# A mixture-of-experts loop skewed by one product, its first weight loads in smaller pieces, and a new ending

## The chip, the core and the metric

The kernel runs on one core of a Trainium2 chip. The core has TensorE for matrix products (the profile calls its matmuls PE and its weight loads PEld), VectorE (DVE), ScalarE (ACT), GpSimd (POOL) and SyncE (SP, which here only issues transfers). The metric is the device time of one execution in microseconds (us), taken as a median of several runs. The engines run side by side and meet at semaphores, so the time is that of the longest chain of waits and not a sum of work.

## What is computed

One layer of a decoder for 256 prompt tokens and 8 x 8 sample tokens, 320 in all, of width 1024. A mixer (a short convolution and four heads of a linear recurrence) comes first, then 32 experts of which each token uses 4, then a last RMSNorm. Cut to what the change touches:

```python
mix = jnp.concatenate([y_conv, o], axis=-1) @ w_out
x = x + mix
# channel mixer, on t = rmsnorm(x)
for e in range(N_EXPERTS):                       # 32
    a = jnp.minimum(t @ w_gate[e] + b_gate[e], SWIGLU_LIMIT)
    u = jnp.clip(t @ w_up[e] + b_up[e], -SWIGLU_LIMIT, SWIGLU_LIMIT)
    hid = (u + 1.0) * a * jax.nn.sigmoid(SWIGLU_ALPHA * a)
    y = y + combine[:, e:e + 1] * (hid @ w_down[e] + b_down[e])
...
y_prompt, y_sample = rmsnorm(x + y, final_norm_w)
```

Every expert has three float32 matrices of 1024 x 1024, 4 MiB each: 96 matrices and 403 MB in all, which the kernel reads once from HBM.

## The kernel before

**Weights.** The matrices go through a ring in SBUF of five places, called groups 0 to 4, of four slots (1 MiB) each. Matrix i goes to group i % 5. Before, i counts gate, up, down of expert 0, then of expert 1, and so on. SP issues all loads in that order from one queue; for matrix i it waits on `wUsed`, which TensorE raises after each quarter of a product, until matrix i-5 (or the half of it) has been used. Matrices 5 to 11 and the last twelve are loaded in halves, the very last in a half and two quarters. The groups overlap older data: group 3 (slots 4 to 7) holds the output projection `w_out` until the mixer's last product, and the end of group 4 holds `mixT`, the mixer's result turned. The first loads therefore wait for the mixer: matrix 0 and 1 on projections that have used their slots (`projMM`), the first half of matrix 4 on `stSMM` and others, matrix 3 and the second half of matrix 4 on `woutMM`, the end of the output projection.

**One expert on TensorE** (lines 1446 to 1476). `product(0, ...)` is gate and `product(1, ...)` is up: 16 float32 products (8 tiles of the contraction by two column halves) at line 1428 after a bias product at line 1411. Inside gate, after its second, third and fourth quarter, stand the three parts of `scatter` (line 1402), which returns the rows of the expert before to their tokens. After up comes `gather` (lines 1319 and 1322), which picks the 64 token rows of the next expert, then the transpose of `hid` (line 1471), `turn_gates` (1384) and `turn` (1390) for the next expert, and last `product(2, ...)`, down, of the same expert.

**Around it.** DVE makes `ga`, `gt`, `gu`, `hid` and adds scattered rows to x (line 985). The output of down is split into three bf16 parts so that `scatter` can be bf16: ACT copies the high part (line 632, `yHigh`), DVE subtracts (991), ACT copies the middle part (634), DVE makes the low part (994).

**The ending** (lines 1495 to 1516, 641 to 655, 1055 to 1062). All engines first pass `further_rounds`, an If that would run more rounds if an expert had over 64 tokens; it isn't taken. Then TensorE scatters the last expert's three parts (1503), spreads `final_norm_w` from `parRows` over all partitions with 32 small products (1511, 1513) and folds the sample tokens' sums (1084). DVE adds (1058) and scales by root and weight (1053). ACT loads the square root's table and makes the squares (648) and the roots (655). SP writes the outputs (400, 403).

Of the kernel before, what the change touches and what calls it, by code (L numbers as in the profile page):

```python
# [5 lines left out]
def hybrid_shortconv_hgrn2_moe_step(nc, A):  # L6
# [9 lines left out]
    D = 1024  # L16
# [29 lines left out]
    ML = 3 * PER_LOOP  # L46
    HALVES_TO, HALVES_FROM = 12, MATS - 12

    def buf(j):

        return (0, 1, 0, 1, 2)[(j - FIRST) % PER_LOOP]

    def buf_before(j):

        return buf(j - 1) if j else buf(E - 1)
# [39 lines left out]
    with ctx:  # L95
# [32 lines left out]
        mixT = view(R2, 0, "p (k t) -> p k t", shape=(8, NT), k=8)  # L128
# [18 lines left out]
        hidT, gt, hid, yrest = ga, gs, gu, xgs  # L147
        ysb = R1[:, 4608:5120].bitcast(bf16).rearrange("p (s d) -> p s d", s=2)
        ysb = [ysb[:, 0, :], ysb[:, 1, :], R4[:, 2400:2656].bitcast(bf16)]
        cv = view(R4, 0, "p (c t) -> p c t", shape=(4, NT), c=4)  # L150
# [4 lines left out]
        PT = R4[:, 1920:2400].bitcast(bf16).rearrange("p (n t) -> p n t", n=3)  # L155
# [15 lines left out]
        gates = sb("gates", [128, 3, 3])  # L171
        rw = sb("rw", [128, 8, E])
        rb = sb("rb", [128, E])
        parRows = sb("parRows", [60, 128])
# [18 lines left out]
        eh = sb("eh", [128, 3, SLOTS], bf16)  # L193
# [7 lines left out]
        endIn = sem("end_in")  # L201
        xIn = [sem(f"x_in{b}") for b in range(3)]
# [7 lines left out]
        woutMM, x2TMM, lgMM, posMM = sem("wout_mm"), sem("x2T_mm"), sem("lg_mm"), sem("pos_mm")  # L210
# [22 lines left out]
        posShift, moeDone, finDone, normed = sem("pos_shift"), sem("moe_done"), sem("fin_done"), sem("normed")  # L233
        lastMM, fnwMM = sem("last_mm"), sem("fnw_mm")
        yHigh, yRest, yMid, yLow = sem("y_high"), sem("y_rest"), sem("y_mid"), sem("y_low")
        aloneP, aloneV, aloneT = sem("alone_pool"), sem("alone_dve"), sem("alone_pe")
# [42 lines left out]
        def further_rounds(eng, one_round, close_round=lambda r: None, rounds=None):  # L279

            rounds = count_of_rounds(eng) if rounds is None else rounds
            with eng.If(rounds > 1):
# [8 lines left out]
                eng.nop()  # L291
            with eng.Else():
                eng.nop()
# [5 lines left out]
        def _(sp):  # L299
# [46 lines left out]
            for i in range(2):  # L346
                for before in range(GROUP_AT[i], GROUP_AT[i] + 4):
                    sp.wait_ge(projMM, load_done(before))
                load_matrix(i, 0, i)
# [5 lines left out]
            load_half(4, 1, 1, 0)  # L355
            sp.wait_ge(s0Out, 16)
            sp.wait_ge(biasDone, 1)
            load_matrix(2, 0, 2)
            sp.wait_ge(woutMM, 3)
            load_matrix(3, 1, 0)  # L360
            load_half(4, 1, 1, 1)

            for i in range(NG_, MATS):
                e, m = i // 3, i % 3
# [15 lines left out]
                if i % ML == 3 * FIRST - 1 and 3 * FIRST < i < MATS - 1:  # L380
                    sp.sem_inc(endIn, 16)

            sp.wait_ge(roundsDone, 1)
            def all_loads(r):
                for i in range(3 * FIRST):
                    sp.wait_ge(wUsed, r * (LPE * E) + 4 * max(0, i - NG_ + 1) + START)
                    load_matrix(i, i // 3, i % 3)
                with sp.Fori(0, LOOPS) as it:
                    for n in range(ML):
                        i = 3 * FIRST + n  # L390
                        sp.wait_ge(wUsed, r * (LPE * E) + it * (4 * ML) + (4 * (i - NG_ + 1) + START))
                        load_matrix(i, it * PER_LOOP + i // 3, i % 3)
                    sp.sem_inc(endIn, 16)

            further_rounds(sp, all_loads)
            yp = A["y_prompt"][0].rearrange("(b p) d -> b p d", p=128)
            ys = A["y_sample"].rearrange("s t d -> (s t) d")
            for b in range(2):
                sp.wait_ge(finDone, b + 1)
                sp.dma_start(yp[b], yout[:, b, :]).then_inc(yOut, 16)  # L400
            sp.wait_ge(finDone, 3)
            for half in range(2):
                sp.dma_start(ys[:, HALF * half:HALF * half + HALF], yout[64 * half:64 * half + 64, 2, 0:HALF]).then_inc(yOut, 16)
# [7 lines left out]
        def _(pool):  # L411
# [22 lines left out]
            def one_round(r):  # L434
# [3 lines left out]
                for j in range(FIRST):  # L438
                    pool.wait_ge(wUsed, r * (LPE * E) + LPE * j + START)
# [1122 lines left out]
```

## Time and profile before

| | |
|---|---|
| median of three runs | 1128.1 us (1128.0 to 1129.16) |
| the profiled execution's own time | 1130.27 us |
| its span | 1128.4 us |
| PE busy | 1103.0 us (98%) |
| DVE, ACT, POOL busy | 394.5, 162.7, 18.2 us |
| moved | 431.67 MB, mean 383 GB/s |
| waits of PE at line 1428 for DMA | 11.7 us |

PE's busy time says that it always had something under way, not that it was at its peak. The slices of the page show where the transfers ran: the first fifth of the span has gaps, and from then on every slice but the last stands near 430 GB/s.

### The profile page before, as it was taken

The page shows a single profiled execution, that of the slowest core. Times are in us where ns is not written, and L with a number is a line of the kernel's source. Part 1 is how long each engine was busy: PE and PEld are TensorE (multiplying, and loading weights), DVE is VectorE, ACT ScalarE, POOL GpSimd, SP SyncE. Part 2 cuts the span into 40 slices and gives each one's busy share as a digit, 9 for nine tenths or more (in the row PEclk, how much of TensorE's full clock was granted, in tenths as well). Part 3 has the DMA queues.
Part 4 walks back from the last instruction along what each step waited for, and adds up shares of the span by engine and source line. Part 5 has one row for each costly group of instructions (what it writes and reads, how often), then busy time and mean ns, then how long its engine had stood idle before and what let it go on. Part 6 is the DMA issues. An engine that isn't in the chain of part 4 may idle for free.

```text
span 1128.4 us, 15518 instructions
## 1 busy us (share of the span) xinstructions
PE 1103.0 (98%) x6341; PEld 454.0 (40%) x6341; DVE 394.5 (35%) x703; ACT 162.7 (14%) x284; POOL 18.2 (2%) x45
## 2 busy tenths in 40 slices
PE   8999999999999999999999999999999999999997
PEld 5657754433333333333333333333333333333333
DVE  4165385433333333333333333333333333233233
ACT  3100124211111111111111111111111111111102
POOL 0002000000000000000000000000000000000000
PEclk9999999999999999999999999999999999999997
DMA  9970247999999999999999999999999999999991
GB/s 323 333 227 22 129 159 298 396 428 427 436 428 430 432 432 433 429 432 433 432 430 432 432 432 432 431 432 432 433 431 431 432 433 429 429 429 428 427 423 63
DMA packets 41442, 431.67 MB, mean 383 GB/s; under 512 B 3809, under 2 KB 23069, under 8 KB 26431
## 3 DMA queue, kind: packets, MB, share of 16 engines
q1 hardware_dynamic: 40592, 430.38, 91.3%
q10 hardware_dynamic: 815, 0.82, 0.2%
q8 instruction: 22, 0.36, 0.1%
q14 instruction: 13, 0.11, 0.0%
HBM read 427.48 MB, written 3.71 MB: 382 GB/s over the span
## 4 chain that ended last, share of the span: by engine, by line
PE 79%; DMA 19%; DVE 1%; ACT 0%; issue 0%; SPq 0%; DVEq 0%
PE ps L1428 47%; DMA ring<-in_w_gate 15%; PE ps L1135 9%; PE ps L1402 5%; DMA ring<-in_w_up 4%; PE ps L1254 3%; PE ps L1319 3%; PE ps L1411 2%; PE ps L1322 1%; PE ps L1390 1%; PE ps L1471 1%; PE ps L1125 1%; PE ps L1384 1%; DMA x<-in_x_sample 0%; PE ps L1511 0%; PE ps L1513 0%
## 5 line engine op out<-in xcount | busy, mean ns | idle before, releaser
L1428 PE MATMUL ps<-ring,RT 128*64 128x512 f32 x3072 | 689.8, 594 | 11.7 <-DMA ring<-in_w_gate 10.3
L1428 PEld LDWEIGHTS ps<-ring,RT 128*64 128x64 f32 x3072 | 210.5, 137 | 410.3 <-issue 381.7
L985 DVE SCALAR_TENSOR_TENSOR x<-ps,gates,x 128x1024 f32<-128x1024 f32 (+1 forms) x93 | 102.9, 1106 | 127.6 <-PE ps L1402 126.5
L1135 PE MATMUL ps<-R,ring 128*128 128x320 f32 x384 | 107.5, 436 | 0.3 <-issue 0.3
L991 DVE TENSOR_TENSOR RT<-ps,R 128x512 f32<-128x512 f32 x32 | 22.1, 692 | 228.9 <-ACT R L632 228.9
L1135 PEld LDWEIGHTS ps<-R,ring 128*128 128x128 f32 x384 | 71.8, 190 | 31.2 <-issue 1.8
L1402 PE MATMUL ps<-R 64*128 64x512 bf16 x558 | 76.8, 381 | 0.0
L1025 DVE TENSOR_SCALAR RT<-ps 128x512 f32<-128x512 f32 x32 | 22.1, 692 | 143.1 <-PE ps L1428 143.1
L624 ACT ACTIVATE RT<-RT 128x512 f32<-128x512 f32 x32 | 20.2, 630 | 300.1 <-DVE RT L1019 300.1
L1402 PEld LDWEIGHTS ps<-R 64*128 64x128 bf16 x558 | 20.8, 98 | 86.0 <-issue 50.3
L603 ACT ACTIVATE RT<-ps 128x512 f32<-128x512 f32 x33 | 19.7, 597 | 237.1 <-PE ps L1322 237.1
L632 ACT ACTIVATE R<-ps 128x512 bf16<-128x512 f32 x32 | 19.1, 597 | 228.3 <-PE ps L1428 228.3
L1319 PE MATMUL ps<-R,P 128*64 128x512 bf16 x396 | 50.6, 389 | 0.0
L973 DVE TENSOR_TENSOR RT<-ps,par 128x512 f32<-128x512 f32 x33 | 22.8, 692 | 67.8 <-PE ps L1390 67.8
L1411 PE MATMUL ps<-R,eh 128*64 128x512 bf16 x192 | 38.9, 401 | 0.2 <-issue 0.2
L1319 PEld LDWEIGHTS ps<-R,P 128*64 128x64 bf16 x396 | 22.2, 109 | 34.7 <-issue 19.3
L1254 PE MATMUL ps<-ring 128*128 128x512 f32 (+1 forms) x96 | 35.9, 598 | 0.0
L1022 DVE TENSOR_TENSOR RT<-RT 128x512 f32<-128x512 f32 x32 | 22.2, 692 | 25.0 <-ACT RT L624 25.0
L994 DVE TENSOR_TENSOR R<-RT,R 128x512 bf16<-128x512 f32 x32 | 22.2, 693 | 22.3 <-ACT R L634 22.3
L1322 PE MATMUL ps<-R,P 128*64 128x256 bf16 x396 | 28.0, 275 | 0.0
L1322 PEld LDWEIGHTS ps<-R,P 128*64 128x64 bf16 x396 | 22.2, 108 | 8.0 <-issue 0.4
L1390 PE MATMUL ps<-consts,RT 128*128 128x128 f32 x132 | 24.7, 310 | 0.0
(226 smaller groups left out, 559.2 us busy)
## 6 DMA issues: line engine op xcount, KB each, us to landing
ring<-in_w_gate SPq DMA_DIRECT2D x26, 4096.0 KB, 32.5
ring<-in_w_up SPq DMA_DIRECT2D x25, 4096.0 KB, 32.0
ring<-in_w_down SPq DMA_DIRECT2D x25, 4096.0 KB, 32.8
ring<-in_w_up SPq DMA_DIRECT2D x14, 2048.0 KB, 39.0
ring<-in_w_down SPq DMA_DIRECT2D x13, 2048.0 KB, 39.8
ring<-in_w_gate SPq DMA_DIRECT2D x12, 2048.0 KB, 40.8
ring<-in_w_in SPq DMA_DIRECT2D x14, 1024.0 KB, 12.7
ring<-in_w_out SPq DMA_DIRECT2D x4, 1024.0 KB, 10.0
```

What stands on the lines that cost most here:

```text
L973: TT(xgT.rearrange("p (c a s) -> p c a s", c=4, a=2), ps[:, 3, :].rearrange("p (c a s) -> p c a s", c=4, a=2), par[:, NG:NG + 8].rearrange ...
L985: STT(xb[b], rows, gates[:, par, b:b + 1], xb[b], ALU.mult, ALU.add).then_inc(accDone, 1)
L994: TT(ysb[2], yrest, ysb[1], ALU.subtract).then_inc(yLow, 1)
L1022: TT(gt, ga, gs, ALU.mult).then_inc(tDone, 1)
L1135: ins = MM(ps[:, n % 2, 0:NT], slot_k(L, 256)[:, k, 128 * half:128 * half + 128], hT[:, k, :], start=(k == 0), stop=(k == KT - 1))
L1254: ins = MM(dst, mixT[:, k, t0:t0 + n], w[:, 512 * half:512 * half + 512], start=(k == 0), stop=(k == KT - 1))
L1319: ins = MM(in_fours(to), P[:, b, 0:SLOTS], half_of(h2p[part][b], half), start=(b == 0 and part == 0), stop=False)
L1322: ins = MM(in_fours(to[:, 256 * at:256 * at + 256]), P[:, 2 + at, 0:SLOTS], half_of(h2p[part][2], half), start=False, stop=(part == 2 and ...
L1390: ins = TR(ps[:, 3, 128 * c:128 * c + 128], fourth(xgs, c), ident)
L1402: ins = MM(to, PT[64 * half:64 * half + 64, par, t0:t0 + n], ysb[part][64 * half:64 * half + 64, :], start=(part == 0), stop=(part == 2))
L1411: MM(shape(ps[64 * half:64 * half + 64, bank, :]), eh[:, buf(j), :], cols(bias3[:, mat, :], half), start=True, stop=False)
L1428: ins = MM(shape(ps[64 * half:64 * half + 64, bank, :]), lhs(k), cols(w, half), start=False, stop=(k == KT - 1))
```

## The change

1. **Order of the matrices** (`I_GATE`, `I_UP`, `I_DOWN`). They are now counted and loaded as gate 0, up 0, gate 1, up 1, down 0, gate 2, up 2, down 1, ..., gate 31, up 31, down 30, down 31.
2. **Skewed loop.** One step on TensorE is gate e and up e with `gather` for e+1, down of expert e-1 with `turn_gates` and `turn` inside it, and the transpose of hid e. The scatter inside gate e is that of expert e-2. ACT, DVE and POOL follow. `hidT`, `gates`, `PT` and `eh` move or have five buffers.
3. **First loads.** Matrix 1 goes in two halves, each as soon as its two slots are free. Matrix 4 (now down 0) has three quarters early and the fourth after the output projection; for this the first two tiles of `mixT` lie elsewhere. Matrix 3 (now up 1) goes in quarters: three as the output projection frees the slots of `w_out` (`woutFree`), one at its end.
4. **Ending.** The last expert's output is copied once in float32 (`yLast`, with `PTLast` for its places) and scattered by 6 float32 products in place of 18 bf16 ones. `final_norm_w` comes by DMA to all partitions, three loads into a free slot. The steps after the rounds stand inside the If, on its first side, and once more after the other rounds.

The core of the diff:

```diff
+    I_GATE, I_UP, I_DOWN = [0] + [3 * j - 1 for j in range(1, E)], [1] + [3 * j for j in range(1, E)], [3 * j + 4 for j in range(E - 1)] + [MATS - 1]
...
-            with eng.If(rounds > 1):
+            with eng.If(rounds < 2):
+                ending()
+                eng.nop()
+            with eng.Else():
...
-            load_half(4, 1, 1, 0)
+            load_half(4, *matrix_of(4), 0)
+            load_quarter(4, *matrix_of(4), 2, lateIn[4])
             sp.wait_ge(s0Out, 16)
             sp.wait_ge(biasDone, 1)
-            load_matrix(2, 0, 2)
+            load_matrix(2, *matrix_of(2))
+            for n, arrived in enumerate((groupIn[3], quarterIn[0], lateIn[3])):
+                sp.wait_ge(woutFree, n + 1)
+                load_quarter(3, *matrix_of(3), n, arrived)
             sp.wait_ge(woutMM, 3)
-            load_matrix(3, 1, 0)
-            load_half(4, 1, 1, 1)
+            load_quarter(3, *matrix_of(3), 3, quarterIn[1])
+            load_quarter(4, *matrix_of(4), 3, quarterIn[2])
...
+                sp.wait_ge(wUsed, 4 * NEXT + START)
+                sp.dma_start(fnw[0], A["final_norm_w"].partition_broadcast(128)).then_inc(fnwIn, 16)
...
+                        gate_up(e, m, j, it, [lambda: None] + [lambda b=b: scatter(b, e2, m2, buf(j - 2)) for b in range(3)] if j > 1 else [])
+                        down(before, j - 1, it, [lambda: turn_gates(after), lambda: turn(after)])
+                        turn_hidden(e)
...
+                down(e0 + (E - 1), E - 1, 0, [lambda b=b: scatter(b, e0 + (E - 2), p0 + (E - 2), buf(E - 2)) for b in range(3)])
+                pe.wait_ge(ptLastOut, r + 1)
+                pe.wait_ge(yHigh, e0 + E + START)
...
+                act.activation(yLast, ps[:, 2, :], ACT.Copy).then_inc(yHigh, 1)
```

**The loop on TensorE.** Before, the second half of one expert, from the bias of up to the end of down (L1428 is a matrix's products, 16 to a matrix; L1319 and L1322 gather; L1471, L1384 and L1390 are transposes):

```order
L1411 MATMUL ps<-R,eh 64x512 x2
L1428 MATMUL ps<-ring,RT 64x512 x16
L1372 REGISTER_ALU
L1319 MATMUL ps<-R,P 64x512 x12
L1322 MATMUL ps<-R,P 64x256 x12
L1471 MATMUL ps<-consts,RT 128x128 x4
L1384 MATMUL ps<-identb,P 128x128 x2
L1384 MATMUL ps<-identb,P 128x64
L1390 MATMUL ps<-consts,RT 128x128 x4
L1411 MATMUL ps<-R,eh 64x512 x2
```

After, the same place, from gather to the transposes of hid (L1382 and L1385 are gather, L1496 the products of down, L1447 and L1453 the two turns, L1534 the transpose of hid):

```order
L1382 MATMUL ps<-R,P 64x512 x12
L1385 MATMUL ps<-R,P 64x256 x12
L1478 MATMUL ps<-R,eh 64x512 x2
L1496 MATMUL ps<-ring,R 64x512 x4
L1447 MATMUL ps<-identb,P 128x128 x2
L1447 MATMUL ps<-identb,P 128x64
L1496 MATMUL ps<-ring,R 64x512 x4
L1453 MATMUL ps<-consts,RT 128x128 x4
L1496 MATMUL ps<-ring,R 64x512 x8
L1534 MATMUL ps<-consts,RT 128x128 x4
```

Down follows gather at once and is broken in two places; the transpose of hid stands behind it.

**The ending on DVE.** Before, the last three adds (L1058) stand behind the way past the If's body:

```order
L1040 TENSOR_SCALAR posm<-posm 128x99
L1041 ISA
L1042 ISA
L285 UNCONDITIONAL_BRANCH
L289 UNCONDITIONAL_BRANCH
L284 REGISTER_ALU
L284 COMPARE_AND_BRANCH
L282 UNCONDITIONAL_BRANCH
L292 UNCONDITIONAL_BRANCH
L1058 SCALAR_TENSOR_TENSOR x<-ps,gates,x 128x1024 x2
L1058 SCALAR_TENSOR_TENSOR x<-ps,gates,x 128x512
L1052 RECIPROCAL st<-st 128x1
```

After, the adds of the last two experts (L1044) come ahead of the one branch, and the scaling (L1120, L1122) right behind it:

```order
L1103 REGISTER_ALU
L1103 COMPARE_AND_BRANCH
L1044 SCALAR_TENSOR_TENSOR x<-ps,R,x 128x1024 x2
L1044 SCALAR_TENSOR_TENSOR x<-ps,R,x 128x512
L1044 SCALAR_TENSOR_TENSOR x<-ps,R,x 128x1024 x2
L1044 SCALAR_TENSOR_TENSOR x<-ps,R,x 128x512
L296 COMPARE_AND_BRANCH
L1120 RECIPROCAL st<-st 128x1
L1122 SCALAR_TENSOR_TENSOR R<-x,st,ring 128x1024
```

The adds moved ahead of the branch, and the weight is read from the ring and no longer from PSUM.

## Rows read from the trace of the kernel before

**Rows 1.** The page: span, and GB/s moved in 40 equal slices of it

```profile
span 1128.4 us, 15518 instructions
GB/s 323 333 227 22 129 159 298 396 428 427 436 428 430 432 432 433 429 432 433 432 430 432 432 432 432 431 432 432 433 431 431 432 433 429 429 429 428 427 423 63
```

**Rows 2.** The chain that ended last: start, length in us, what; middle of the span

```profile
660.09 6.87 PE ps L1428 x32
...
687.81 6.87 PE ps L1428 x32
...
750.43 41.31 DMA ring<-in_w_gate
...
808.71 41.32 DMA ring<-in_w_gate
```

**Rows 3.** Timeline of SP's issues, 150 to 225 us: start, length, line, destination and source

```profile
177.16 0.33 SPq L304 DMA_DIRECT2D ring<-in_w_down  x1
198.16 0.33 SPq L304 DMA_DIRECT2D ring<-in_w_gate  x1
198.60 0.37 SPq L311 DMA_DIRECT2D ring<-in_w_up  x1
212.60 3.76 SPq L311 DMA_DIRECT2D ring<-in_w_down  x2
```

**Rows 4.** Windows around the first product: length; engines' busy us; last: clock, DMA share, GB/s

```profile
198.00:212.60 14.60, 13.66 (x117) 6.83 (x117) 9.59 (x32) 6.81 (x14) 0.00 (x0) 1.00 0.92 380
212.60:232.00 19.40, 19.40 (x111) 8.44 (x109) 4.29 (x9) 2.15 (x4) 0.00 (x0) 1.00 1.01 429
```

**Rows 5.** Timeline of PE at the first product of expert 0

```profile
208.95 3.62 PE L1428 MATMUL ps<-ring,RT 128*64 128x512 f32 x16
```

**Rows 6.** Line 316, the issue of the last quarter, and its time to landing

```profile
L316 SPq DMA_DIRECT2D ring<-in_w_down x1: 3887/3887/3887, 1059.2 to 1059.2; - x1
...
DMA to landing us min/median/max: 44.3/44.3/44.3
```

**Rows 7.** Timeline of PE in gate of expert 31, where it last waits for gate's second half

```profile
1083.96 1.51 PE L1428 MATMUL ps<-ring,RT 128*64 128x512 f32 x6 [0.48 <-DMA ring<-in_w_gate]
```

**Rows 8.** The chain that ended last, experts 29 and 31, with PE's last wait at 1093.76

```profile
1025.79 0.76 PE ps L1402 x6
1026.54 1.87 PE ps L1428 x8
...
1093.76 3.65 PE ps L1428 x16
1097.42 1.36 PE ps L1319 x12
...
1099.45 0.68 PE ps L1471 x4
1100.13 0.24 PE ps L1384 x3
...
1101.39 6.89 PE ps L1428 x32
```

**Rows 9.** Timeline of all engines in the ending, with idle time before in brackets

```profile
1108.31 0.60 ACT L632 ACTIVATE R<-ps 128x512 bf16<-128x512 f32 x1 [7.13 <-PE ps L1428]
...
1111.06 1.28 ACT L572 ACT_TABLE_LOAD   x1 [0.77 <-issue]
...
1113.67 3.13 DVE L1058 SCALAR_TENSOR_TENSOR x<-ps,gates,x 128x1024 f32<-128x1024 f32 x3 [2.53 <-issue]
...
1114.99 1.06 ACT L648 ACTIVATE R<-x 128x1024 f32<-128x1024 f32 x1 [2.43 <-DVE x L1058]
...
1121.27 0.16 DVE L1052 RECIPROCAL st<-st 128x1 f32<-128x1 f32 x1 [4.46 <-PE ps L1513]
...
1124.24 0.75 DVE L1053 SCALAR_TENSOR_TENSOR R<-x,st,ps 128x512 f32<-128x512 f32 x1
1125.02 1.21 SPq L403 DMA_DIRECT2D y_sample<-R  x2
```

More of the change, by code:

```diff
@@ L201, in hybrid_shortconv_hgrn2_moe_step @@
         endIn = sem("end_in")
+        quarterIn = [sem(f"quarter_in{n}") for n in range(3)]
         xIn = [sem(f"x_in{b}") for b in range(3)]
@@ L290, in further_rounds @@
                         eng.nop()
-                eng.nop()
-            with eng.Else():
+                ending()
                 eng.nop()
@@ L404, in _ @@
+            further_rounds(sp, all_loads, ending=outputs)
             sp.wait_ge(yOut, 64)
@@ L1065, in _ @@
+            further_rounds(dve, one_round, rounds=rounds[0], ending=scales)
         @block.tensor
@@ L1078, in _ @@
             pe.wait_ge(parIn, 16)
[L1079 removed]
+            TR(ps[:, 0, 0:52], parRows[:], ident[0:52, 0:52]).then_inc(parMM, 1)
             def sum_halves(column, out):
@@ L1445, in one_round, with gate_up, down @@
                     stay_busy(3)
+                def gate_up(e, m, j, it, between=()):
+                    pe.wait_ge(ehDone, m + 1 + START)
+                    pe.wait_ge(xgTOut, m + 1 + START)
+                    pe.wait_ge(aDone, e + START)
+                    product(0, half_c(xgT), I_GATE[j], it, buf(j), between)
+                    pe.wait_ge(uDone, e + START)
+                    product(1, half_c(xgT), I_UP[j], it, buf(j))
+                    gather(m + 1)
+                def down(e, j, it, between):
+                    pe.wait_ge(yRest, e + START)
+                    product(2, half_c(hidT), I_DOWN[j], it, buf(j), between, operand=(hidTOut, e + 1 + START))
@@ L1446, in experts, with turn_hidden @@
+                def turn_hidden(e):
+                    pe.wait_ge(hidDone, e + 1 + START)
+                    pe.wait_ge(hidTOut, e + START)
+                    for c in range(4):
+                        ins = TR(ps[:, 4, 128 * c:128 * c + 128], fourth(hid, c), ident)
+                    ins.then_inc(hidTMM, 1)
+                gate_up(e0, p0, 0, 0)
+                turn_hidden(e0)
+                turn_gates(p0 + 1)
+                turn(p0 + 1)
                 def experts(it, these):
                     for j in these:
-                        e = e0 + (it * PER_LOOP + j)
@@ L1461, in experts @@
-                        pe.wait_ge(xgTOut, m + START)
-                        pe.wait_ge(aDone, e + START)
-                        product(0, 0, half_c(xgT), e, it, j, [lambda: None] + [lambda b=b: scatter_before(b) for b in range(3)]
-                                if not isinstance(e, int) or e > 0 else [])
-                        pe.wait_ge(uDone, e + START)
-                        product(1, 1, half_c(xgT), e, it, j)
-                        gather(m)
-                        pe.wait_ge(hidDone, e + 1 + START)
@@ L1469, in experts @@
-                        pe.wait_ge(hidTOut, e + START)
-                        for c in range(4):
-                            ins = TR(ps[:, 4, 128 * c:128 * c + 128], fourth(hid, c), ident)
-                        ins.then_inc(hidTMM, 1)
-                        turn_gates(m)
-                        turn(m)
-                        pe.wait_ge(yRest, e + START)
-                        product(2, 2, half_c(hidT), e, it, j, operand=(hidTOut, e + 1 + START))
-                experts(0, range(FIRST))
+                        e, m = e0 + (it * PER_LOOP + j), p0 + (it * PER_LOOP + j)
@@ L1507, in _ @@
-            FN = 52
-            for k in range(D // 128):
-                row = ident[0:FN + 8, FN + k:FN + k + 1]
-                at = 128 * (k % 4)
-                MM(ps[:, 4 + k // 4, at:at + 128], row.broadcast_to([FN + 8, 128]), parRows[:], start=True, stop=True)
-                half = slice(64 * (k // 4), 64 * (k // 4) + 64)
-                ins = MM(ps[half, 2, at:at + 128], row.broadcast_to([FN + 8, 64]), parRows[:], start=True, stop=True)
-            ins.then_inc(fnwMM, 1)
-            pe.wait_ge(finSq, 3)
```

328 lines of the change are left out of this document (180 added, 148 removed).

## The prediction

> **What bounds the kernel now.** I read the page's GB/s line first. 96 matrices of 4.19 MB are 403 MB of the 432 MB moved, and from the ninth slice to the last but one the line stands at 423 to 436 [rows 1]: up to about 1101 us the transfers don't pause. The page's PE line says 98% busy as well, so the next view is the chain, to see who waits. In its middle one expert follows another after 687.81 - 660.09 = 27.72 us with no DMA piece: there TensorE waits for nothing and eats what the ring holds. From 750 us on the chain runs through loads, and two of its DMA pieces that lie six matrices apart are 58.28 us apart [rows 2], 9.71 us a matrix, 29.14 an expert, 4.19 MB / 9.71 = 432 GB/s. So TensorE is 1.4 us an expert faster than the stream, lives off the ring for 500 us and then waits for the stream. The end is set by (a) when the stream starts for good, (b) 91 matrices at its rate, (c) what comes after the last of them.
>
> **Part 1: earlier first loads, worth 0.7 us and not 10.** The diff brings 1 MiB of matrix 4 and 3 MiB of matrix 3 forward into the idle stretch before 198 us. Taken alone that is 4.19 MB / 0.43 = 9.7 us of stream. But the ring has five places, and matrix 5 can only be asked for when TensorE has used half of matrix 0. Before, that issue is at 212.60 [rows 3], 3.65 us after the first product began at 208.95 [rows 5], and that product waits for the routing, not for weights. The loads issued at 198.16 and 198.60 are 6.29 MB; by 212.6 they had moved 14.6 us x 380 GB/s = 5.55 MB [rows 4], so 0.74 MB were left, 1.7 us at 429 GB/s. The stream before was thus only 1.7 us behind "all five places full". After, the places are full some microseconds early, the stream stops, and starts anew at 212.6. How long a start takes I bound from the same row: 5.55 MB at 429 GB/s take 12.9 us of the 14.4 since the issue, so 1.5 us at most, and no less than 0; I take 1.0, nearer the top since the row also has a slow stretch. Everything behind it, the last landing included, comes 1.7 - 1.0 = 0.7 us earlier (0.2 to 1.7). Issue work on SP is 0.33 us for each added load [rows 3], with nothing behind it until 212.6. The skewed order frees the places at nearly the same times: first half of matrix 2 used at about 231 us, while the queue then holds work until 232.8. That margin is thin, and a bubble costs about what it lasts.
>
> The Trainium skill, page "DMA: Bandwidth & Descriptors", section "Specifications", gives about 0.6 us to the first byte on this path; by it the restart is at 213.2 and the shift 1.1 us in place of 0.7.
>
> **Part 2: the skewed loop, dearer for TensorE by 0.3 us an expert, free up to 0.45.** It removes no instruction. Chains that it stretches out (`hid`, `hidT`, the three-way split) weren't waited for before: no such piece stands in the chain's middle. What it adds is that down is broken twice. A quarter of a product is 6.87 / 4 = 1.72 us, but one that follows a scatter takes 1.87 [rows 8]. Two more such entries are 2 x 0.15 = 0.30 us; from below it is 0, if transposes do not cost what scatters do, and from above three entries at 0.17, 0.5. Pace 28.02 us, still under 29.14. Before, expert 1 starts at 208.7 + 27.7 - 2.6 = 233.8 us (expert 0 has no scatter), and 31 experts x 27.72 would have ended at 1093.1, against the real 1108.3: 15.2 us spare. The new order takes 30 x 0.30 = 9.0 of them, and about 1.8 for a later gate 1 and the new end: 4.4 us, 0.15 an expert, are left. So the price is nothing on the path, covered by the stream; if that cover is used up, each further 0.1 us an expert costs 3 us.
>
> **Part 3: where TensorE ends.** The last wait before is for the second half of expert 31's up, at 1093.76, and down ends at 1101.39 + 6.89 = 1108.28 [rows 8]. After, the order of arrival is up 31, down 30, down 31. The place that up 31's second half takes in the stream is the one that gate 31's had, which let PE go on at 1083.96 [rows 7], now 0.7 earlier, 1083.3. Then, from rows 8: second half of up 3.65; gather 2.03; bias 0.23; down 30 with its turns 6.87 + 0.24 + 0.68 + 0.30 = 8.09: it ends at 1097.3. Its output copy (0.60 on ACT [rows 9]) and the hidden copy after the transpose (0.68, then 0.60) must end before down 31 starts: 1.5 us. Down 31 carries the scatter of expert 30 in it: 4 quarters of 1.87 and 3 scatters of 0.76, 9.76. **End 1108.5**, 0.2 later than before. The last quarter lands at 1059.2 + 44.3 = 1103.5 [rows 6] and is needed at 1106.6, so it isn't what is waited for.
>
> **Part 4: the ending, -8.1 us.** Before [rows 9]: the adds start at 1113.67, after 2.53 us in which DVE had nothing to wait for (the way past the If), though the first scatter part was there near 1112. They end at 1116.8. Then DVE idles 4.46 us for the 32 small products of `final_norm_w` (L1513), and scales from 1121.27 to 1124.99; 3.4 us later the span ends. After: `yLast` copy 0.63, to 1109.1; first pair of the float32 scatter 1.0 (the 8 pairs of a matrix take 6.87 us, 0.86 a pair [rows 8], and about 0.15 until DVE sees it; 1.9 if this pair doesn't overlap as those do), to 1110.1; adds 3.13, to 1113.3; the branch not taken 0.15; scaling 3.72, to 1117.1; outputs 3.4: **1120.5**. That is the 4.46 us of idle removed, the adds 3.5 us earlier, less 0.15. What is late next: ACT's first root. Copy end 1109.1, 0.77 issue, table 1.28 and its small use 0.2: 1111.4; square and root take 1.5, 1112.9, half a microsecond before DVE asks. The norm's weights (0.79 MB, 1.8 us) queue behind the last quarter and land at about 1105.5, needed at 1113.4.
>
> Unknown is what the branch costs DVE. Bounds: 0.1, and the 2.53 of rows 9. I take the low end, since the new code stands right behind the branch as the order shows, where the old stood beyond the body. The Trainium skill, "Runtime: NRT & Kernel Launch", section "Instruction fetch mechanics", says that a taken branch out of the fetched window stalls for a fetch; the 2.53 us agree with it, and by it the new branch is free, while SP's jump after its last issue falls beside the outputs' flight.
>
> **The sum.** Span 1128.4 + 0.2 - 8.1 = 1120.5. The execution shown took 1130.27 by its own time, with a span of 1128.4; the median of runs is 1128.1, 0.3 under that span, so I forecast 1128.1 - 7.9 = 1120.2 us.
>
> **The rivals.**
> A. *The early loads pay in full.* If the stream at 212.6 had as much backlog as was brought forward, 9.7 us would come off the stream, but TensorE's spare of part 2 lets only 4.4 of them through: 1120.2 - 4.4 = 1116. Against it: the 0.74 MB left by rows 4. 5%.
> B. *TensorE becomes the bound.* Entries at 0.17 and one more of them (pace 28.2) or small waits eat the 4.4 us spare; at 28.3 the end moves by (0.58 - 0.45) x 30 = 4 us: 1124. For it: the spare is thin. 15%.
> C. *The gain of the ending is half.* The branch or the float32 scatter cost DVE 2.5 us more: 1122.7. 10%.
> D. *Slower: a wait once an expert.* `down(e-1)`, `turn_hidden(e)` and the next gate stand in a row; should gate e+1 have to wait for `xgT`, or its scatter for the low part of the split, by w us each time, the loss is (w - 0.15) x 30. From w = 0.41 on the whole gain is gone, at w = 0.8 the time is 1139. Against it: from the end of down the split takes 0.6 + 0.75 + 0.6 + 0.7 us in sequence with the hidden copy between, some 2.8, and the scatter comes 4.4 us after it. 7%.
> E. *No change.* A bubble near 232 us or at the first whole-matrix load (about 280 us) of some 3 us, with B: 1126 to 1129. 8%.
> Forecast: 55%, with a range of its own of 1118.5 to 1122.5.
>
> **How the numbers follow.** B, C and the forecast lie between 1117.5 and 1124.5 and hold 80%. A little of A reaches down to 1116. The range is 1116.5 to 1125. Faster by over 0.2% (under 1125.8) is the forecast, A, B, C: 85%; within 0.2%, about what a measurement of this kernel can tell from no change: 7%; slower 8%.
>
> **What would show it.** Right: in the changed profile SP's first issue of matrix 5 is still at 212.6, with a hole in GB/s just before it; the pace in the middle is near 28.0; the chain meets DMA pieces later than 750 us, perhaps only from 1000 us on; the last product ends near 1108.5; DVE's idle time before the scaling is under 0.5 us. Wrong: a pace over 28.2, any PE wait for ACT or DVE inside the loop, a GB/s slice under 420 after 212 us, or 2 us of DVE idle between adds and scaling.

## The result, and the profile after

The changed kernel takes 1169.4 us (median of four runs, 1165.5 to 1171.4) against 1128.6 us before (four runs): a ratio of 1.035, 95% interval 1.032 to 1.038. I had forecast 1120.2 and a range of 1116.5 to 1125.0. It is slower by 41 us, and outside of the range. Times here are medians and ratios compare undisturbed runs alone; one run of all, an execution of the written-out loop below, took 5953 us at a mean granted clock of 0.17 and is in no ratio.

The page of after, cut to its span, the engines, the granted clock, the transfers in 40 slices, the queue that carries instructions (packets, MB, share of 16 engines) and the chain by engine:

```profile
span 1169.8 us, 15420 instructions
PE 1126.1 (96%) x6303; PEld 453.7 (39%) x6303; DVE 393.2 (34%) x700; ACT 165.8 (14%) x284; POOL 18.1 (2%) x45
PEclk9999999999999899998999999999999999899998
GB/s 327 325 201 90 126 214 359 307 429 427 429 433 431 425 385 430 429 434 429 378 432 429 433 432 380 430 431 431 433 376 427 432 431 429 410 430 426 428 140 47
q8 instruction: 66, 1.08, 0.4%
PE 95%; issue 3%; DVE 1%; DMA 0%; ACT 0%; SPq 0%; DVEq 0%
```

Before, the GB/s line stood near 430 to its end [rows 1]. Now it has dents at equal distances, four to between 376 and 385 and a fifth to 410, and the chain holds practically no DMA: TensorE and not the stream sets the end. PE's busy time is 23 us longer than before, though its trace has fewer matmuls (6303 against 6341). The view of waits of PE in after (line, what ended the wait: us in total, times, longest) names the idle part:

```profile
PE ps L1478 <- issue: 14.8, 7, 3.0
PE ps L1496 <- issue: 12.0, 5, 2.7
```

"Issue" is time in which the engine waited for nothing that the profile shows. L1478 is the bias of a product and L1496 the products, and the chain shows where it happens (start, length, what):

```profile
392.97 0.68 PE ps L1534 x4
393.66 2.44 issue
396.10 0.64 PE ps L1478 x2
396.74 2.89 PE ps L1496 x6
399.63 2.58 issue
402.20 4.43 PE ps L1496 x10
406.63 0.75 PE ps L1469 x6
```

L1534 is the last instruction of the loop's body, L1478 the first of the next turn. So the pair of stalls stands at the return from the end of the loop's code to its head. The loop has five experts in its body and returns five times (its stalls begin at 393.66, 543.51, 693.42, 843.27 and 993.49 us). The 16 products around the second stall (6 ahead of it, 10 behind) take 2.89 + 4.43 = 7.32 us, the stall not counted, where 16 that follow without a break take 3.43 [rows 8 has 6.89 for 32]. The windows say why (length; PE, PEld, DVE, ACT, POOL busy; last the granted clock, the DMA share and GB/s), after first, then before:

```profile
240.00:393.00 153.00, 153.00 (x851) 55.19 (x847) 46.16 (x74) 18.48 (x32) 1.18 (x5) 1.00 1.00 429
393.00:410.00 17.00, 11.98 (x44) 3.80 (x46) 3.41 (x6) 1.82 (x3) 0.00 (x0) 0.80 0.97 415
410.00:543.00 133.00, 133.00 (x737) 47.62 (x736) 40.69 (x64) 15.74 (x28) 1.18 (x5) 1.00 0.99 422
```

```profile
393.00:410.00 17.00, 17.00 (x90) 5.19 (x89) 5.39 (x8) 1.52 (x3) 0.24 (x1) 1.00 1.00 430
```

The granted clock is full before the return and means 0.80 over the 17 us around it: after its idle 2.4 us TensorE runs for a while at the lower of its two levels (1.2 in place of 2.4 GHz). In windows of 1 us it is 0.50 from 396 to 399 us, 1.00 in the second gap, 0.50 again from 403 to 405, and 1.00 from 406 on. From the first return to the fifth are 4 x 149.96 us; five experts at the pace between returns, 28.13 us, are 140.65. A return thus costs 149.96 - 140.65 = 9.3 us. Of the 14.8 + 12.0 us of waits above all but some 1.0 (what the kernels without stalls show in the same row) stand at returns, 5.2 us each; the other 4.1 are the lower clock. Five returns cost 46.5.

Why before has none of it is in the page's row for q8, the queue that carries instructions. Before, it reads

```profile
q8 instruction: 22, 0.36, 0.1%
```

and after 66 packets with 1.08 MB: 44 more, nearly 9 for each return. The times of the packets say where they belong. In windows of 1 us, after has its nine of the first return at 393, 399, 407, 424, 448, 472, 493, 516 and 537 us: the first two lie at the two stalls, and from 424 us on they are 21 to 24 us apart, all through the loop's code. Before has none between 390 and 1095 us. The code of the loop is fetched anew at each return; before, it wasn't.

What I looked for in the changed profile was otherwise there: SP asks for matrix 5 at 212.51 us (forecast 212.6), with a hole of 50 GB/s from 205 to 210 just before; the pace between returns is 28.13 us (28.02).

### The profile page after: what moved, and what is told of

It is laid out like the page before. It is cut to its first block, busy times and chain, and to the rows that moved or that the text cites. A ratio compares the mean times of both kernels' runs of the same rounds, so it can differ in the third digit from the quotient of the medians.

```text
span 1169.8 us, 15420 instructions
## 1 busy us (share of the span) xinstructions
PE 1126.1 (96%) x6303; PEld 453.7 (39%) x6303; DVE 393.2 (34%) x700; ACT 165.8 (14%) x284; POOL 18.1 (2%) x45
## 3 DMA queue, kind: packets, MB, share of 16 engines
q8 instruction: 66, 1.08, 0.4%
## 4 chain that ended last, share of the span: by engine, by line
PE 95%; issue 3%; DVE 1%; DMA 0%; ACT 0%; SPq 0%; DVEq 0%
PE ps L1496 60%; PE ps L1196 9%; PE ps L1469 6%; PE ps L1382 4%; PE ps L1315 3%; PE ps L1478 3%; PE ps L1385 2%; PE ps L1453 2%; PE ps L1534 2%; PE ps L1186 1%; PE ps L1447 1%; DMA x<-in_x_prompt 0%; PE ps L1224 0%; DVE R L1122 0%; DVE x L1044 0%
## 5 line engine op out<-in xcount | busy, mean ns | idle before, releaser
L1496 PE MATMUL ps<-ring,RT 128*64 128x512 f32 x2048 | 483.6, 609 | 12.0 <-issue 12.0
L1496 PEld LDWEIGHTS ps<-ring,RT 128*64 128x64 f32 x2048 | 146.6, 139 | 278.6 <-issue 272.9
L1496 PE MATMUL ps<-ring,R 128*64 128x512 f32 x1024 | 239.5, 598 | 0.0
L1044 DVE SCALAR_TENSOR_TENSOR x<-ps,R,x 128x1024 f32<-128x1024 f32 (+1 forms) x96 | 106.2, 1106 | 190.4 <-PE ps L1469 187.1
L1496 PEld LDWEIGHTS ps<-ring,R 128*64 128x64 f32 x1024 | 67.8, 136 | 99.2 <-issue 92.0
L648 ACT ACTIVATE RT<-RT 128x512 f32<-128x512 f32 x32 | 20.1, 630 | 358.7 <-DVE RT L1078 358.7
L1050 DVE TENSOR_TENSOR RT<-ps,R 128x512 f32<-128x512 f32 x31 | 21.5, 692 | 109.5 <-ACT R L676 109.5
L1478 PE MATMUL ps<-R,eh 128*64 128x512 bf16 x192 | 40.1, 412 | 15.5 <-issue 14.8
L1382 PE MATMUL ps<-R,P 128*64 128x512 bf16 x396 | 50.3, 387 | 0.0
L1382 PEld LDWEIGHTS ps<-R,P 128*64 128x64 bf16 x396 | 22.9, 109 | 33.7 <-issue 19.1
L1053 DVE TENSOR_TENSOR R<-RT,R 128x512 bf16<-128x512 f32 x31 | 21.4, 692 | 21.6 <-ACT R L679 21.6
L1453 PEld LDWEIGHTS ps<-consts,RT 128*128 128x128 f32 x132 | 18.5, 210 | 25.5 <-issue 25.1
L1385 PE MATMUL ps<-R,P 128*64 128x256 bf16 x396 | 28.1, 274 | 0.0
```

The costliest lines, as they stand in the source:

```text
L1044: STT(xb[b], rows, gates[:, par, b:b + 1], xb[b], ALU.mult, ALU.add).then_inc(accDone, 1)
L1382: ins = MM(in_fours(to), P[:, b, 0:SLOTS], half_of(h2p[part][b], half), start=(b == 0 and part == 0), stop=False)
L1385: ins = MM(in_fours(to[:, 256 * at:256 * at + 256]), P[:, 2 + at, 0:SLOTS], half_of(h2p[part][2], half), start=False, stop=(part == 2 and ...
L1453: ins = TR(ps[:, 3, 128 * c:128 * c + 128], fourth(xgs, c), ident)
L1478: MM(shape(ps[64 * half:64 * half + 64, mat, :]), eh[:, par, :], cols(bias3[:, mat, :], half), start=True, stop=False)
L1496: ins = MM(shape(ps[64 * half:64 * half + 64, mat, :]), lhs(k), cols(w, half), start=False, stop=(k == KT - 1))
```

## The experiments

**What the theories differ in.** The body of the loop is nearly the same size in both kernels (1612 instructions on TensorE after, 1613 before, counted in the compiled program with a product and its weight load as two; the traces, which leave out waits and register work, have 1551 of them in one turn of after). What differs is how many stand ahead of it: 3355 before, 3246 after. *Theory P*: where the loop's code lies in instruction memory decides whether a return has to fetch. *Rival Q* (theory S in the first four expectations): something in the new body or the new stream does it, such as the way that the skewed order meets the loads. I give the place as the number ahead modulo 256: 27 before, 174 after. The count itself stands in no trace, and the 256 was a supposition.

**After, moved to the place of before.** 109 instructions that only count a semaphore up, at the start of TensorE's work.

```diff
+            for _ in range(109):
+                pe.sem_inc(padS, 1)
             pe.wait_ge(busyOut, 1)
             keep_busy(8)
```

> The changed kernel with 109 semaphore increments on TensorE at its very start, so that the loop's first instruction stands where it stands in the kernel before, counted modulo 256 instructions. In the changed kernel's trace TensorE stands still about 2.4 and 2.6 us at each of the five returns to the loop's head and then runs at half clock for some 5 us, 9.2 us a return, 46 us in all. Theory P (place: whether the loop's body stays in TensorE's instruction memory depends on where it begins): no stall at the returns, about 1169.4 - 46, limited from below by the stream: 1120 to 1126 us. Theory S (the skewed order itself, with its other waits and its emptier DMA queue, makes the return dear): the place changes nothing, 1165 to 1172 us.

Measured: 1139.6 us, ratio 1.0082 (1.0065 to 1.0099), 22 instruction packets, and no stall in the loop. The increments themselves are dear, as PE's waits show (L1135 is `keep_busy`, TensorE's first products):

```profile
PE ps L1135 <- issue: 18.4, 1, 18.4
```

They push SP's first issue of matrix 5 to 228.14 us, 15.6 later. Without that the span of 1138.4 would be 1122.8. By its time the run lies between what P and its rival expected, since I had not priced the increments; by the stalls and the packets P holds: the same loop, the same order of loads, other place, no stalls.

**Before, moved to the place of after.** The same with 147 increments in the kernel before.

> The kernel before with 147 semaphore increments on TensorE at its start, which puts its loop where the changed kernel has it (modulo 256). Nothing else is changed. Theory P: five returns of about 9.2 us each appear, less the 15 us by which TensorE alone would be done ahead of the stream: 1128 + 46 - 15 = 1159 us, 1150 to 1165. Theory S: 1128 to 1130 us, the kernel before.

Measured: 1183.6 us, ratio 1.0475 (1.0457 to 1.0492), 67 packets. The waits of PE:

```profile
PE ps L1074 <- issue: 24.3, 1, 24.3
PE ps L1431 <- issue: 16.2, 5, 3.8
PE ps L1414 <- issue: 13.7, 6, 3.0
```

The old loop (L1414 bias, L1431 products) now stalls at all five returns. The time is above the 1150 to 1165 us that I had expected, again by the increments: less the start's delay of 21.6 us the span is 1160.7, near the 1159 of P. Nothing of the change is in this kernel, so Q falls.

**After, with fewer increments.** 40 in place of 109, place 214.

> The changed kernel with 40 semaphore increments on TensorE at its start. By my count of instructions the loop then begins at 214 of 256 and, 1612 long, still reaches over eight pieces of 256, as from where it stands in the changed kernel if about 7 or more instructions precede my count. Theory P: still 1165 to 1172 us, five stalled returns. If any added instruction cured it: 1120 to 1126. Theory S: 1165 to 1172 as well.

Measured: 1129.4 us, span 1127.6, 21 packets, no stall. I had expected stalls here; my idea of which places are bad was wrong, the idea that the place decides was not.

**After, with the first round's loop written out.** No return, thus nothing to fetch twice; the cost is more code.

```diff
-                        if (i, k) in EARLY and isinstance(r, int) and isinstance(it, int):
+                        if (i, k) in EARLY and isinstance(r, int) and isinstance(it, int) and it == 0:
...
-                with pe.Fori(0, LOOPS) as it:
-                    experts(it, range(FIRST, FIRST + PER_LOOP))
+                if isinstance(r, int):
+                    for it in range(LOOPS):
+                        experts(it, range(FIRST, FIRST + PER_LOOP))
+                else:
+                    ...
```

> The changed kernel with TensorE's loop written out for the first round (six times its body, no return to a head); the other engines keep their loops. Theory P: no stall anywhere in the experts, 1120 to 1126 us, the same as with the loop well placed. Theory S: if the stalls come from the order of work and not from the return, they stay at the same places, 1165 to 1172 us. A third way: written out, TensorE must fetch new code all the time and could stall oftener, over 1130 us.

Measured: 1131.3 us (ten runs), ratio 1.0021 (1.0011 to 1.0031), no stall, 52 packets. It isn't the cure: from 833 us on its chain goes through loads,

```profile
890.24 41.96 DMA ring<-in_w_gate
949.17 41.96 DMA ring<-in_w_gate
```

58.93 us for six matrices, 9.82 a matrix, where before needs 9.71 [rows 2]. For 91 matrices this 1% would be 10 us. What takes it from the stream stays open: the fetched code alone is too little, 0.85 MB against 0.36 before, 1.1 us at 430 GB/s.

**A cheap way to move the loop.** 24 products of eight columns behind `keep_busy(8)`, 48 instructions, place 222.

```diff
             keep_busy(8)
+            for _ in range(24):
+                MM(ps[:, 1, 0:8], busy[:, 0:128], busy[:, 128:136], start=True, stop=True)
```

> The changed kernel with 24 products of 8 columns (48 instructions, as I count them) on TensorE right after its first warm-up products, where it waits for the first data anyway. The increments of the earlier runs cost 0.18 us each and pushed the start by 4.4 and 15.6 us; these should cost nothing. Theory P (the loop's place): the loop begins at 222 of my count, near the 214 that ran without stalls, so no stalls, and the time is that of the change by itself: the span of the run with 40 increments less its later start, 1127.6 - 4.4 = 1123.2, so 1123 us. Had the cure been the later start and not the place: 1165 to 1172 us.

Measured: 1125.4 us, ratio 0.9965 (0.9952 to 0.9979), span 1124.4, 21 packets. SP's first issue of matrix 5 is at 213.88 us, 1.4 later than in after, but a part of that can't be the products': it is at 213.24 in the kernel with the loop written out, which has none of them. This is the change without its accident, and it is 0.35% faster than the kernel before.

**The same, with both turns behind the last quarter of down and SP's outputs outside the If.** It asks whether the two re-entries of part 2 and SP's jump cost anything.

> As the run with 24 small products, and two edits: the two turns stand behind down's last quarter in place of within it, and SP's output loads and stores come after the If and not inside it, so that its way past the If's body is done before it has to issue. In the profiles with the new ending the span ends 4.5 to 5.7 us after the last store is issued, against 3.4 before. Theory: the pace falls from 28.13 to about 27.8 us, which brings at most the 0.5 us by which TensorE is later than the stream allows, and the end comes 1 to 2 us sooner: 1121 to 1122 us. Rival: what lengthens the end is the store itself, and the time stays at 1123.

Measured: 1125.45 us, 0.9967 (0.9955 to 0.9979): nothing gained, where I had expected 1121 to 1122. With shorter steps on TensorE the chain goes through loads again, the last product ends at 1109.79 instead of 1110.10, and the end comes 5.2 us after the last issue of an output, 5.1 before that edit.

**The same, without the early loads.** From the kernel with 24 small products; matrix 3 and the third quarter of matrix 4 are issued only after the output projection.

```diff
-            load_quarter(4, *matrix_of(4), 2, lateIn[4])
             ...
-            for n, arrived in enumerate((groupIn[3], quarterIn[0], lateIn[3])):
-                sp.wait_ge(woutFree, n + 1)
-                load_quarter(3, *matrix_of(3), n, arrived)
             sp.wait_ge(woutMM, 3)
+            load_quarter(4, *matrix_of(4), 2, lateIn[4])
+            for n, arrived in enumerate((groupIn[3], quarterIn[0], lateIn[3])):
+                load_quarter(3, *matrix_of(3), n, arrived)
```

> As the run with 24 small products, but the third quarter of matrix 4 and all quarters of matrix 3 are issued after the output projection, as the kernel before did with the same bytes. Forecast of the prediction: the stream can't go on before matrix 5 is asked for anyway, so this costs 0.7 us (0.2 to 1.7): 1123 to 1125 us. Rival: the 4 MiB brought forward are worth their full 9.7 us, 1128 to 1133 us.

Measured: 1126.4 us, 0.9973 (0.9964 to 0.9983). The early loads are worth 1.0 us by the medians, with intervals that overlap; from the first issue of matrix 5 to the last product the profiled runs have 1110.10 - 213.88 = 896.2 us with them and 1110.15 - 212.57 = 897.6 without. 9.7 is ruled out.

**The same, with the scaling behind the If on DVE**, as in the kernel before.

```diff
-            further_rounds(dve, one_round, rounds=rounds[0], ending=scales)
+            further_rounds(dve, one_round, rounds=rounds[0])
+            scales()
```

> The kernel after with the 24 small products at the start (1125.41 us, span 1124.4, in which the last product of the prompt ended at 1110.10 = T0, the sample's scaling ran on VectorE from T0 + 5.42 to T0 + 9.14, and the profile ended at T0 + 14.3), and with the scaling of the outputs written behind the if of the further rounds on VectorE, as in the kernel before; nothing else is changed. Theory F, the forecast's price for the branch past the code of a further round: VectorE stands for about 2.5 us between the sample's additions and its scaling (the gap was 2.6 us in the kernel before), so that the scaling begins at about T0 + 7.9, the span is 1126.9 and the time 1127.9. Theory N, the branch costs nothing here because the additions end no earlier than the code is there: scaling from T0 + 5.4, span 1124.4 within 0.5.

Measured (one run): 1127.9 us, span 1126.1; T0, the end of the last product, is 1109.38. DVE in the ending, here and then with the scaling inside the If, where T0 is 1110.10:

```profile
1111.34 3.53 DVE L1044 SCALAR_TENSOR_TENSOR x<-ps,R,x 128x1024 f32<-128x1024 f32 x3 [3.05 <-PE ps L1568]
1117.20 0.16 DVE L1120 RECIPROCAL st<-st 128x1 f32<-128x1 f32 x1 [2.33 <-ACT st L706]
```

```profile
1112.07 3.53 DVE L1044 SCALAR_TENSOR_TENSOR x<-ps,R,x 128x1024 f32<-128x1024 f32 x3 [3.05 <-PE ps L1567]
1115.52 0.15 DVE L1120 RECIPROCAL st<-st 128x1 f32<-128x1 f32 x1
```

The scaling begins at T0 + 7.8 against T0 + 5.4 with it inside the If. The profile puts the 2.33 us down to ACT's root, but ACT had it ready from 1114.14 on (0.29 us from 1113.85), three microseconds earlier. Only the place of the scaling differs between the two kernels, so what was late is the way past the If. Theory F holds: 2.4 us on DVE, near the 2.53 of rows 9.

**Which places stall.** Five more kernels only move the loop, by small products as above; each ran once, as the one with 40 increments did, and is read by its trace.

> The kernel before with 59 small products (118 instructions) at the same idle place. By the runs so far the loop stalls when it begins at 174 of my count and not at 27 or 214; with a body of 1612 and pieces of 256 instructions that means that between 42 and 81 instructions precede my count, and that places 138 to 174 all stall. This one begins at 145. Theory P: five stalled returns and three times the instruction fetches (about 66 in place of 22), 1128 + 46 - 15 = 1159 us. If only some narrow place is bad, or the small products do no harm: 1128 us.

> The kernel after with 12 small products (24 instructions) at the start on TensorE: by my count the loop then begins at 198 of 256, between 174, where all five returns stall, and 214 and 222, where none does. Theory P' (what decides is where the loop's code lies in instruction memory, and the places that stall form one stretch that ends between 174 and 214): either all five returns stall (span about 1169 with 66 instruction packets), or some of them do, as at 145 (one return, 8 packets more and about 6 to 9 us), or none (span 1124 with 21 or 22 packets); the number of packets above 22 is 8 or 9 for each return that stalls. Theory Q (the small products help by something else than their number of instructions, such as the half-microsecond later start): no stalled return and span 1124 whatever the place. The run splits the two only if returns stall; otherwise it narrows the stretch to 174 to 198.

> The kernel after with 6 small products (12 instructions) at the start: by my count the loop begins at 186 of 256, 12 instructions behind the place where all five returns stall (174), 12 ahead of one where none does (198). Theory P' says only that the number of instructions ahead of the loop decides; so the outcome is one of three: all five returns stall (span about 1168, 60 or more packets), one or two do (span 1130 to 1141, 30 to 39 packets), or none (span 1122 to 1124, 21 or 22 packets). If the stretch that stalls ends sharply, the packets are either 21 or 60 and more. The rival to P', that a later or busier start of TensorE heals the loop, expects none too, and would be the better explanation only if 186 is clean at once; then as few as 12 instructions undo 45 us either way.

> The kernel before with 66 small products (132 instructions) ahead on TensorE; its loop then begins at 159 of 256. Theory W (the loop stalls where it touches eight blocks of code, a stretch 76 wide from about 110 to 198): all five returns stall, 62 or more instruction packets, span 1128.4 + 37 to 41 = 1165 to 1170. Rival V (an edge that is soft, with 145 on it): one to three stalled returns, 30 to 48 packets, span 1130 to 1152. Rival U (the stretch is narrow, and begins behind 159): no stalled return, 22 packets, span 1129.

> The kernel before with 41 small products (82 instructions) ahead on TensorE; its loop then begins at 109 of 256, just outside the stretch of 110 to 198 of theory W. Theory W: no stalled return, 22 packets, span 1129. If instead some returns stall (30 or more packets, span 1130 or more), the stretch reaches lower than 76 places allow, and the count of blocks is not what decides. Rivals U and V expect none either.

With those from above:

| kernel | instructions ahead | mod 256 | returns that stall | packets | span, us |
|---|---|---|---|---|---|
| after | 3246 | 174 | 5 | 66 | 1169.8 |
| after, 6 products | 3258 | 186 | 5 | 66 | 1173.9 |
| after, 12 products | 3270 | 198 | 0 | 21 | 1122.6 |
| after, 40 increments | 3286 | 214 | 0 | 21 | 1127.6 |
| after, 24 products | 3294 | 222 | 0 | 21 | 1124.4 |
| before | 3355 | 27 | 0 | 22 | 1128.4 |
| after, 109 increments | 3355 | 27 | 0 | 22 | 1138.4 |
| before, 41 products | 3437 | 109 | 0 | 21 | 1128.7 |
| before, 59 products | 3473 | 145 | 1, the first | 30 | 1129.4 |
| before, 66 products | 3487 | 159 | 1, the first | 30 | 1130.5 |
| before, 147 increments | 3502 | 174 | 5 | 67 | 1182.3 |

Twelve instructions decide about 50 us: the kernel with 6 small products is the slowest of after's, the one with 12 the fastest. The rival that a busier or later start heals the loop falls with the first of them, and with the kernel before under 147 increments, which starts later still and stalls. In the chain of the kernel with 6, the return reads

```profile
393.63 2.75 issue
396.38 0.64 PE ps L1480 x2
397.02 5.15 issue
402.17 5.61 PE ps L1498 x16
```

The edge above is sharp, between 186 and 198. The lower one is soft: nothing at 109, the first return alone at 145 and 159, all five at 174. I had expected all five at 145 and named all five first for 159; both were wrong. A stalled return has 9 packets, 8 in the kernels with one. A packet carries 1.08 MB / 66 = 16.4 KB.

The Trainium skill, page "Runtime: NRT & Kernel Launch", section "Instruction fetch mechanics", says that code comes in blocks of 16 KiB (256 instructions), that TensorE's instruction memory has 128 KiB, thus eight blocks, and that a taken branch to a target outside the current window of two pages has to wait for a fetch. The packets agree with the block in size, and in their distance of 21 to 24 us from 424 on: 256 of the 1612 instructions, which take 140.65 us, take 22.3. That the period of the places is just 256 is not pinned down by these eleven kernels; it agrees with them (174 stalls in both, at 3246 and at 3502 ahead). By the page's figures 1612 instructions touch seven or eight blocks, eight from a stretch of starts 75 wide. As an estimate, with its upper end laid between 186 and 198, it begins between 112 and 123, which takes in every place that stalled and none that didn't. For that some 58 to 69 instructions would have to precede my count, which no run shows. Why 145 and 159 recover after one return and why a return fetches nine blocks aren't explained by it and stay open. The page also says that fetching ahead is purely sequential and that there is no instruction cache to profit from; by that each of the five returns would fetch. Here kernels with 21 or 22 packets returned five times with no fetch at all, so the measurement decides.

**The version that beats both, timed.** After with 12 small products, in six runs.

> The kernel after with 12 small products (24 instructions) at the start on TensorE (loop start 198 of 256 by my count), the kernel of the one look at 1124.42 us, now timed against the kernel before. Theory P' (nothing is left of the stalls): 1124.4 within 0.7, a ratio of 0.9960 to 0.9967, no stalled return, 21 or 22 instruction packets; below the kernel with 24 such products (1125.41) by 0.5 to 1.0 because TensorE starts half a microsecond or more earlier. The rival: the one look was at the lucky end of a spread, and the time is that of the kernel with 24 products, 1125.4 within 0.4.

Measured: 1124.4 us (six runs, 1123.7 to 1125.7), ratio 0.9954 (0.9942 to 0.9966): 0.5% faster than the kernel before. Its return, in the window that held after's stalls:

```profile
393.00:410.00 17.00, 17.00 (x90) 5.63 (x90) 6.74 (x10) 2.45 (x4) 0.24 (x1) 1.00 1.00 432
```

## Why the prediction was wrong, point by point

**The step that failed** is none of the sum's terms but one that was missing. Part 2 says of the skewed loop that "it removes no instruction" and costs TensorE 0.3 us an expert; the first part says that between experts TensorE "waits for nothing". Both were read inside the body. The change also takes 109 instructions out ahead of the loop, and the return to its head was never priced. It was free before only because of where the code lay. Its price is 5 x 9.3 = 46.5 us; the last product ends at 1154.95 in after and at 1107.83 with 12 small products ahead, 47.1 apart. Part 4 even quotes the rule on branches and the 2.53 us of rows 9, and applies both to the If alone. The row that could have raised the question stood in the page of before: 22 packets in q8 for a kernel that returns five times.

No rival had it. D, the slower one, put a wait into each expert and would have shown as PE waiting for DVE or ACT; B had TensorE as the bound at 1124. Two of the "wrong" signs did appear: GB/s slices under 420, and, with the returns counted in, a pace of 149.96 / 5 = 29.99 us over the 28.2. (D's own sum gives 1139.7 at w = 0.8, not 1139.)

For the rest I compare with the kernel with 12 small products, where the stalls are gone.

- **Part 1, early loads, 0.7 us:** 1.0 by the medians and 1.4 by the profiled runs, inside the 0.2 to 1.7, though the times' intervals don't exclude zero; the hole and the unmoved issue of matrix 5 are as forecast. The stream started again 0.9 us after the issue (212.64, first bytes after 213.4), where I took 1.0. Rival A fell.
- **Part 2, pace 28.02:** 28.13 measured. One quarter that follows a turn takes 1.87 as assumed; the turn of the gates grew from 0.24 to 0.35 [rows 8]. I left 0.15 us an expert as spare, and 28.13 used nearly all of it. From 252.46 to 1068.25 us, where the transposes of hid begin for experts 1 and 30, 29 steps of 28.13 follow without a single DMA piece, where I expected some from 1000 us on. TensorE and the stream tie: in the other profile of this same kernel (1122.6 us) DMA has 8% of the chain. Rival B came true as a mechanism, its price was near zero. The kernel with the shorter steps shows the other side of the tie.
- **Part 3, last product ends at 1108.5:** 1107.83, near, but not by the way that I gave. I built it on the moment when a load lets TensorE go on in up 31. There TensorE waits for no load: up 31 ends at 1085.96 by its own pace, 1.0 before the 1083.3 + 3.65 of the forecast. Between down 30 and down 31 lie 1.40 us (transpose, then 0.7 of wait for DVE's L1050), where I had 1.5. That both ways end within 0.7 us is the tie, and partly luck.
- **Part 4, ending:** too cheap by 2.5 us. Forecast from last product to the end of the span 12.0 us, measured 1122.3 - 1107.83 = 14.5, in after 14.85; before 20.1. Its steps in after, where the last product ends at 1154.95:

```profile
1155.70 1.14 PE ps L1565 x4
...
1156.92 1.30 DVE x L1044
...
1159.84 0.53 issue
1160.37 0.17 DVE st L1120
...
1163.35 0.75 DVE R L1122
```

The adds begin 1.97 us after the last product (forecast 1.6) and take 3.53 in place of 3.13, so that the scaling starts at 5.4 and not at 4.9. The 0.53 of issue in the chain is not idle time: DVE's timeline has the last add until 1160.45 and shows no gap before L1120, so the branch not taken (0.15 in the forecast) cost nothing that can be seen. Scaling takes the 3.7 expected. Most of the rest is behind it: from the last output's issue to the end are 5.3 us with 12 products (1117.00 to 1122.3), 3.4 before [rows 9]. SP's own last wait, for y_sample to land, is 2.3 us, 1.6 before. With SP's outputs out of the If the 5.2 us remained, so its jump isn't the cause; what lengthens the end stays open. What I had left unknown, the branch's price on DVE, was taken right at its low end. Rival C had the same 2.5 us, but on DVE ahead of the outputs, which isn't where they are.
- **The sum.** Without the stalls the kernel takes 1124.4, inside my range, 4.2 over the forecast. That it is rival B's number is chance. Of these 2.5 are the ending, less 0.7 for the last product; 2.1 lie in how a span becomes a time: I took the median as 0.3 under the span, since it was so for the execution shown before, while this one takes 1124.08 with a span of 1122.3, 1.8 over it; and 0.3 is its median over its profiled run. The kernel before had 1129.7 as its median on that chip, 1.6 over the one I started from, so the gain to compare with my 7.9 is 5.3 us.

## What to carry to other kernels

A loop need not be free at its back edge, the jump from its end to its head: when a change adds or removes instructions ahead of a large loop, compare the instruction packets in the page before and after, and look at the chain at each return. If there are stalls, move the loop by a few dozen cheap instructions and measure again before judging the change itself. A range made from the terms of a sum doesn't cover a step that isn't in the sum.

## What the runs showed of the hardware

- A return to a loop's head on TensorE cost either nothing or 9.3 us (in after: two gaps, 2.4 and 2.6 us at the first return, and products at the lower clock), by the place of a body of 1612 instructions alone; 12 instructions decide between spans of 1173.9 and 1122.6 us.
- After such a return the whole body is fetched again, a packet of 16.4 KB each 21 to 24 us; a kernel whose returns don't stall had no instruction packet from 390 to 1095 us. Where only the first return stalled (145, 159), the span was 0.7 to 1.8 us over that of the same kernel at 109.
- A semaphore increment on TensorE took about 0.155 us: the idle time at the start is 7.8 us with 40, 18.4 with 109 and 24.3 with 147. As padding, small products are cheaper: with 12 of them SP's first issue of matrix 5 is at 212.5 to 212.6 us as without any, with 24 it is up to 1.4 us later.
- The way past the If's body cost DVE 2.4 us between adds and scaling; with the scaling inside the If, on the side that is taken, there was no gap.
- TensorE's granted clock was 1.00 up to a return that stalls and 0.80 in the 17 us from it, with gaps of 2.44 and 2.58 us. In the kernel with 6 small products the gaps are 2.75 and 5.15 us, and 16 products take 5.61 us where 3.43 is the full rate.
